# Gathering chosen tokens from a token-major copy: feature order, read stride, and fills on TensorE

## The chip, the cores and the metric

The kernel runs as one program on one core of a Trainium2 chip. The metric is the time of one execution on the device in microseconds. Three runs of the kernel before took 1545.58, 1551.16 and 1552.26 us (median 1551.16). TensorE's clock is granted at one of two levels, 1.2 and 2.4 GHz; a profile shows the second as 1.00 and the first as 0.50.

## The reference

A block of two layers on 256 tokens of 1024 features, all in fp32. The first layer mixes tokens (a gated scan in two directions, a spatial gate, an output projection) and then sends tokens through 16 experts by expert choice:

```python
def moe_expert_choice(h, router_w, w_gate, w_up, w_down):
    B_, T, _ = h.shape
    cap = CAPACITY_FACTOR * T // N_EXPERTS          # 2 * 256 / 16 = 32
    aff = jax.nn.softmax((h @ router_w).astype(jnp.float32), axis=-1)
    gate, idx = lax.top_k(jnp.swapaxes(aff, 1, 2), cap)
    xs = h[bidx, idx]
    hid = jax.nn.silu(jnp.einsum('becd,edf->becf', xs, w_gate)) * jnp.einsum('becd,edf->becf', xs, w_up)
    ye = jnp.einsum('becf,efd->becd', hid, w_down) * gate[..., None].astype(h.dtype)
    return jnp.zeros_like(h).at[bidx, idx].add(ye)
```

`w_gate`, `w_up` and `w_down` are 16 x 1024 x 2048 (or its transpose) each: 8 MB for each expert and matrix, some 403 MB in all. The second layer (a linear-attention branch, a convolution branch, an output projection and a gated extra input) follows.

## The kernel before

Activations are kept by features: feature on the partition, token on the free axis. The projections of both layers are done as three products in a rounded format (weights and activations split into a high and a low part); the experts, the gathers and the scatters are plain fp32, for which the profile has two records a product.

Between the first layer's output projection and the experts lies the choice. `routed(k)` (L1955) computes the logits of the 16 experts and transposes the tokens' features block by block into four PSUM banks, so that a token lies on a partition. ScalarE copies these banks to SBUF, scaled by each token's norm, as `H2k` (L719, four copies of 128x512). VectorE computes the softmax (`affk`, L1260 to L1270), TensorE transposes it (L2057), VectorE takes the 32 largest values of each expert in four rounds and counts them through (L1274 to L1284, event "ranks"), TensorE transposes the ranks back (L2066), and VectorE writes one-hot matrices `Pm` that say which token goes to which of an expert's 32 places (L1291, L1295). In between TensorE has products of its own to do, which belong to the second layer (`pp_products`, L2035): eight records ahead of the transposes of the softmax and 24 behind them. The latter start only when the third copy of `H2k` has emptied its bank, since they write to that bank. Two products without a use, `keep_on(2)` (L2029), stand behind the transposes of the ranks.

The gathers are matrix products: stationary is a 128x128 piece of `H2k` (128 tokens, 128 features), moving is `Pm`. There are eight blocks k of 128 features, and two token halves i:

```python
mm = e.matmul(B[b][:, 0:32], H2k[:, i, 512 * (k // 4) + k % 4:512 * (k // 4) + 512:4], Pm[:, i, 0, :], ...)
```

The slice ends in `:4`: block k takes every fourth feature of a range of 512, because the rows of the expert weights are loaded so that each partition holds four neighbouring rows. The columns of the piece are 16 bytes apart. `gather_first(k)` gathers for expert 0 alone (32 columns), `gather(0, k)` for experts 1 to 7 (224 columns), `gather(1, k)` for experts 8 to 15 (256). ScalarE takes each result to `XS` (L723, L728).

`up(x, m, b)` (L2116) does eight steps k for expert x and matrix m (0 gate, 1 up): four products of 32 stationary columns and 512 moving columns, one for each quarter of 2048 outputs, side by side on the array (eight records). For x = 0, m = 0 each step first issues `gather_first(k + 1)`; for x = 0 and x = 1 with m = 1 each step first issues `gather(x, k)`. The down products (L2165) follow the transposes of `hid`.

The weights come on one queue, issued by SyncE in the order of `LOADS` (L309). The first 20 tiles of 1 MB (24 tiles make an expert: 8 gate, 8 up, 8 down) are loaded ahead of the experts, as far as there is room. Each later load waits until the last tile that lay in its place has been used (`p_exp`, L491): the load of tiles 20 and 21 waits for tile 1, that of 22 and 23 for tile 3, that of 24 and 25 for tile 7, that of 26 and 27 for tile 9, and so on round the ring. Engines have their orders written out by hand, and semaphores join them.

Of the kernel before, what the change touches and what calls it, by code (L numbers as in the profile page):

```python
# [11 lines left out]
ACT = mybir.ActivationFunctionType  # L12
# [52 lines left out]
def program(nc, a, out):  # L65
    ctx = ExitStack()
    with ctx:
        names = []

        def signal(name, step=1):  # L70
            names.append(Signal(ctx.enter_context(nc.semaphore(name)), step))
            return names[-1]
# [7 lines left out]
        def put(name, n, at=None, dtype=F32):  # L80
            o = pos[0] if at is None else at
            if at is None:
                pos[0] = o + (n + 7) // 8 * 8
            assert o + n <= TOT, (name, o, n)
            return nc.alloc_sbuf_tensor_at(name, [128, n], dtype, offset=arena + 4 * o)[:, :]
# [11 lines left out]
        B = [ctx.enter_context(nc.psum_tensor(f"B{i}", [128, 512], F32))[:, :] for i in range(8)]  # L97
# [72 lines left out]
        ffs, ffp, lgb, rsc = put("ffs", 16), put("ffp", 16), put("lgb", 16), put("rsc", 8)  # L170
# [3 lines left out]
        H2k = v2(put("h2k", 2048, page(13)))  # L174
# [3 lines left out]
        Pm = put("pick", 1024).rearrange("p (i e s) -> p i e s", i=2, e=16)  # L178
# [156 lines left out]
        def expert_src(t, n):  # L335
# [49 lines left out]
        a_step, a_hi, a_left, a_sig, a_h, a_lvl, a_norm, a_moe = (signal(n) for n in (  # L385
            "act_step", "act_hi", "act_left_bank", "act_sigmoid", "act_h", "act_level", "act_norm", "act_moe"))
# [126 lines left out]
        def scalar(e):  # L513
# [202 lines left out]
            for c in range(2):  # L716
                for i in range(2):
                    e.wait_ge(*p_misc.at("xt", c))
                    e.activation(H2k[:, i, 512 * c:512 * c + 512], B[2 * c + i], ACT.Copy, scale=rsc[:, i:i + 1]).then_inc(*a_left("h2k", c, i))  # L719

            def gather_first(k):
                e.wait_ge(*p_misc.at("gather first", k))
# [946 lines left out]
        def tensor(e):  # L1669
            left = {}  # L1670

            def bank(b):

                if b in left:
                    e.wait_ge(*left.pop(b))
                return B[b]

            def next_bank(*key):
                b = UNIT_BANK[key]
                return bank(b), b  # L1680
# [24 lines left out]
            def mm3(ps, n, cols, ah, al, kn=8, w_first=True, ready=None):  # L1705

                wh, wl = kn_(hi_(n), n)[:, :, cols], kn_(lo_(n), n)[:, :, cols]
                if n >= SECOND and ready is None:
                    e.wait_ge(*v_lo.at(n))
                    for k in range(kn):  # L1710
                        for j, (w, x) in enumerate(((wh, ah), (wh, al), (wl, ah))):
                            mm = e.matmul(ps, w[:, k, :], x(k), start=k == 0 and j == 0, stop=k == kn - 1 and j == 2)  # L1712
                    return mm
                e.wait_ge(*a_hi.at(n))
                for k in range(kn):
                    if ready is not None:
                        e.wait_ge(*ready(k))
                    for j, x in enumerate((ah, al)):
                        l, r = (wh[:, k, :], x(k)) if w_first else (x(k), wh[:, k, :])
                        e.matmul(ps, l, r, start=k == 0 and j == 0, stop=False)  # L1720
                e.wait_ge(*v_lo.at(n))
                for k in range(kn):
                    l, r = (wl[:, k, :], ah(k)) if w_first else (ah(k), wl[:, k, :])
                    mm = e.matmul(ps, l, r, start=False, stop=k == kn - 1)  # L1724
                return mm

            half = lambda j: slice(128 * j, 128 * j + 128)
# [24 lines left out]
            ps, b = next_bank("q", 0)  # L1752
# [3 lines left out]
            for k in range(8):  # L1756
                e.wait_ge(*v_h.at("lo", 0, k))
                for j in range(2):
                    for i, (w, x) in enumerate(((wh, hx), (wh, hxl), (wl, hx))):
                        mm = e.matmul(ps[:, 256 * j:256 * j + 256], w[:, k, half(j)], x(k), start=k == 0 and j == 0 and i == 0, stop=k == 7 and j == 1 and i == 2)  # L1760
# [13 lines left out]
            for h in range(2):  # L1774
                for k in range(8):
                    mm = e.matmul(two_banks[h], wl[:, k, half(h)], HTh[:, k, :], start=False, stop=k == 7)
# [3 lines left out]
            for d in range(2):  # L1780
                for h in range(4):
# [3 lines left out]
                    ps, b = next_bank("f", d, h)  # L1785
# [106 lines left out]
            for h in range(4):  # L1892
# [10 lines left out]
                mm = e.matmul(po, vx[:, 1, half(h)], PT[:, 1, h, :], start=False, stop=True)  # L1903
# [10 lines left out]
            for g in range(4):  # L1914
# [5 lines left out]
                for i in range(2):  # L1920
                    o0 = 256 * (g % 2) + 128 * i
                    mm = e.matmul(B[4 + g // 2][:, o0:o0 + 128], svt[:, i, half(g)], wst[:, g, :], start=True, stop=True)
# [8 lines left out]
            for b_ in range(4):  # L1931
                for hf in range(4):
                    mm = e.matmul(B[4][32 * hf:32 * hf + 32, 0:16].rearrange("p (m q b) -> p b m q", m=2, b=4)[:, b_], ident[:, b_::4],
                                  ffs.rearrange("p (m q h) -> p h m q", m=2, h=4)[:, hf], start=True, stop=True)
# [5 lines left out]
            for c in range(2):  # L1940
                for name, xh, xl in (("a", oTh, oTl), ("b", uTh, uTl)):
# [3 lines left out]
                    for hf in range(2):  # L1945
                        ps, b = next_bank(name, c, hf)
                        for j in range(2):
                            mm = mm3(ps[:, 256 * j:256 * j + 256], n, half(2 * hf + j), lambda k: xh[:, k, :], lambda k: xl[:, k, :], kn=4)
# [29 lines left out]
            for c in range(4):  # L1978
                n = NO["wo", c]
                if c == 0:  # L1980

                    ps, b = next_bank("wo", 0)
                    e.wait_ge(*v_lo.at(n))
                    wh, wl = kn_(hi_(n), n), kn_(lo_(n), n)
                    for ks in (range(6), (6, 7)):
                        for j in range(2):
                            for k in ks:
# [5 lines left out]
                                mm = e.matmul(pj, wl[:, k, half(j)], mh(k), start=False, stop=k == 7 and j == 1)  # L1993
# [4 lines left out]
                else:  # L1998

                    ps, b = next_bank("wo", 3)  # L2000
# [8 lines left out]
                    for k in range(8):  # L2009
                        mm = e.matmul(ps, wl[:, k, half(1)], mh(k), start=False, stop=k == 7)  # L2010
# [18 lines left out]
            def keep_on(times, b=7):  # L2029

                bank(b)
                for _ in range(times):
                    e.matmul(B[b][:, 0:128], ident, ident, start=True, stop=True)

            def pp_products(c, k):  # L2035
                if k == 0:
                    bank(pp_bank[c])
                for db in (2 * c, 2 * c + 1):
                    pp_product(db, k)

            def pp_product(db, k):
                b = pp_bank[db // 2]
                mm = e.matmul(B[b][:, 256 * (db % 2):256 * (db % 2) + 256], wpp[:, k, half(db)], pT[k], start=k == 0 and db % 2 == 0, stop=k == 1 and db % 2 == 1)
                if k == 0 and db == 7:
                    mm.then_inc(*p_misc("pp", "upper rows"))
                if k == 1 and db % 2:
                    mm.then_inc(*p_misc("pp", db // 2))
                    left[b] = a_left.at("pp", db // 2)
# [2 lines left out]
            e.wait_ge(*l_pT.at(1))  # L2051
            for k in range(2):
                pp_products(0, k)
            bank(5)
            e.wait_ge(*v_moe.at("aff"))
            for i in range(2):
                mm = e.transpose(B[5][0:16, half(i)], affk[:, i, :], ident)  # L2057
            mm.then_inc(*p_misc("aff"))
            left[5] = v_left.at("aff")
            for k in range(2):  # L2060
                for c in range(1, 4):
                    pp_products(c, k)
            e.wait_ge(*v_moe.at("ranks"))
            bank(4)
            for i in range(2):
                mm = e.transpose(B[4][:, 16 * i:16 * i + 16], af[0:16, half(i)], ident[0:16, 0:16])  # L2066
# [4 lines left out]
            def gather_first(k):  # L2071
                b = first_bank(k)
                bank(b)
                if k == 0:
                    e.wait_ge(*v_moe.at("pick first"))
                    e.wait_ge(*a_left.at("h2k", 1, 1))
                for i in range(2):
                    mm = e.matmul(B[b][:, 0:32], H2k[:, i, 512 * (k // 4) + k % 4:512 * (k // 4) + 512:4], Pm[:, i, 0, :], start=i == 0, stop=i == 1)
                mm.then_inc(*p_misc("gather first", k))
                left[b] = a_moe.at("xs first", k)  # L2080

            def gather(hf, k):
                b, c0 = gather_bank(hf, k), 0 if hf else 32
                bank(b)
                if k == 0:
                    e.wait_ge(*v_moe.at("pick", hf, 1))
                for i in range(2):
                    mm = e.matmul(B[b][:, 0:256 - c0], H2k[:, i, 512 * (k // 4) + k % 4:512 * (k // 4) + 512:4], Pm[:, i, 8 * hf + c0 // 32:8 * hf + 8, :], start=i == 0, stop=i == 1)  # L2088
                mm.then_inc(*p_misc("gather", hf, k))
                left[b] = a_moe.at("xs", hf, k)  # L2090

# [43 lines left out]
            for x in range(NE):  # L2135
# [4 lines left out]
                for i in range(2):  # L2140
                    mm = e.transpose(B[7][:, half(i)], PR[:, i, :, :].rearrange("p r s -> p (r s)"), ident)  # L2141
# [6 lines left out]
                for c in range(4):  # L2148
                    mm = e.transpose(B[2][:, half(c)], hid[:, c::4], ident)  # L2149
# [5 lines left out]
                for j in range(4):  # L2155
# [5 lines left out]
                    for i, part in enumerate(parts):  # L2161
                        if t + i == load_of[t][0] or len(parts) == 2:
                            e.wait_ge(*(l_last.at() if i < len(parts) - 1 else landed[tile_page(t)].at("expert", t + i)))
                        for db, c, r in part:
                            mm = e.matmul(B[3 + db][32 * r:32 * r + 32, :], hidT[:, 128 * c + 32 * j:128 * c + 32 * j + 32],  # L2165
                                          v2(tile_at_page(t + c // 2))[:, c % 2, 512 * db:512 * db + 512], start=j == 0, stop=j == 3)
# [201 lines left out]
        for f in (sync, scalar, vector, gpsimd, tensor):  # L2368
            f(Counting())
# [8 lines left out]
        @block.scalar  # L2378
        def _(eng):
            scalar(eng)  # L2380
# [55 lines left out]
```

## Time and profile before

| | |
|---|---|
| Median of three runs | 1551.16 us |
| Profiled execution's own time | 1552.23 us |
| Its span (first to last instruction) | 1550.4 us |
| TensorE matmul busy | 1211.2 us (78%) |
| TensorE weight loads busy | 757.2 us (49%) |
| VectorE, ScalarE, GpSimd busy | 562.5, 423.9, 30.0 us |
| Mean granted clock of TensorE | 0.874 |
| Read from memory | 518.66 MB, 335 GB/s over the span |

Times in the rows below are counted from the span's start. PE is TensorE's matmuls, PEld its weight loads (they run beside matmuls), DVE VectorE, ACT ScalarE, POOL GpSimd, SPq SyncE's queue. L719 is line 719 of the kernel. "B<-pick,h2k" names what an instruction writes and reads. A record of a matmul lasts from its start until its result has drained, so that records overlap; the pace of a row of them is read from the chain of waits or from the starts.

### The profile page before, as it was taken

Reading aid. Unit: us, or ns where it says so; the run is one execution under the profiler, and the core shown is the slowest. Engines: PE = TensorE matmul, PEld = TensorE weight load, DVE = VectorE, ACT = ScalarE, POOL = GpSimd, SP = SyncE. Lnnn points to the kernel's source line nnn. Section 1 sums busy time; section 2 is a strip of 40 time slices with the busy share of each in tenths; the row PEclk is TensorE's granted clock in tenths of the full one; section 3 lists DMA queues with packets and bytes.
Section 4 is the critical chain, followed back from the end, with each engine's and each line's share of the span. In section 5 each row is a group of like instructions: output and inputs, shape, how many; then the busy total and the mean of one; then the engine's idle time right before and its main releaser. Section 6 shows DMA issues by size and latency. Waiting matters only on the chain.

```text
span 1550.4 us, 18533 instructions
## 1 busy us (share of the span) xinstructions
PE 1211.2 (78%) x8124; PEld 757.2 (49%) x8124; DVE 562.5 (36%) x829; ACT 423.9 (27%) x553; POOL 30.0 (2%) x36
## 2 busy tenths in 40 slices
PE   4999999999666756666756656656656899999998
PEld 1878899854212212212211212212212589999997
DVE  4887776511101101101101101101101497777566
ACT  2865656222100000000000000000000454467545
POOL 0012000000000000000000000000000000000000
PEclk7999999979968777867878787878878999999999
DMA  9646868769999999999999999999999855555551
GB/s 364 215 156 224 298 221 332 299 249 424 432 431 431 432 432 431 430 431 431 431 431 430 432 432 432 431 429 430 432 432 427 328 164 163 162 182 184 184 186 55
DMA packets 106479, 520.90 MB, mean 336 GB/s; under 512 B 5904, under 2 KB 83728, under 8 KB 89376
## 3 DMA queue, kind: packets, MB, share of 16 engines
q1 hardware_dynamic: 106256, 519.63, 83.3%
q8 instruction: 64, 1.05, 0.3%
q14 instruction: 15, 0.12, 0.0%
q10 hardware_dynamic: 144, 0.09, 0.0%
HBM read 518.66 MB, written 1.05 MB: 335 GB/s over the span
## 4 chain that ended last, share of the span: by engine, by line
PE 49%; DMA 47%; DVE 1%; ACT 1%; SPq 1%; issue 1%; DVEq 0%
PE B L1712 16%; DMA four<-in_wd 15%; DMA four<-in_wu 15%; DMA four<-in_wg 13%; PE B L2130 8%; PE B L1720 6%; PE B L2165 3%; PE B L1724 3%; PE B L1839 2%; DMA wslot<-in_w_in 2%; PE B L2088 1%; DMA aslot<-in_ada_w 1%; PE B L1690 1%; PE B L1827 1%; PE B L1842 1%; DMA wslot<-in_w_out 1%
## 5 line engine op out<-in xcount | busy, mean ns | idle before, releaser
L2130 PE MATMUL B<-four,xs 128*32 128x512 f32 x1824 | 294.7, 804 | 197.9 <-DMA four<-in_wu 132.5
L2130 PEld LDWEIGHTS B<-four,xs 128*32 128x32 f32 x1824 | 73.4, 141 | 398.4 <-issue 323.5
L2165 PE MATMUL B<-four,hidT 128*32 128x512 f32 x896 | 153.2, 846 | 88.0 <-DMA four<-in_wd 87.4
L1712 PE MATMUL B<-hnh,whj 128*128 128x256 f32 x488 | 138.1, 283 | 0.0
L1712 PE MATMUL B<-hnh,wslot_r 128*128 128x256 f32 x488 | 137.6, 282 | 0.0
L1712 PE MATMUL B<-hn_r,whj 128*128 128x256 f32 x488 | 137.1, 281 | 0.0
L2165 PEld LDWEIGHTS B<-four,hidT 128*32 128x32 f32 x896 | 37.0, 148 | 193.5 <-issue 121.7
L970 DVE TENSOR_TENSOR wslot_r<-wslot,whj 128x2048 fp32r<-128x2048 f32 x52 | 118.8, 2288 | 31.4 <-ACT whj L524 31.3
L524 ACT ACTIVATE whj<-wslot 128x2048 fp32r<-128x2048 f32 x51 | 97.3, 1913 | 87.6 <-PE B L1712 82.0
L1324 DVE TENSOR_TENSOR hid<-sgm,B 128x512 f32<-128x512 f32 x16 | 11.0, 688 | 281.5 <-PE B L2130 281.5
L1304 DVE SCALAR_TENSOR_TENSOR x<-B,mod,x 128x256 f32<-128x256 f32 x128 | 55.9, 479 | 152.6 <-PE B L2106 152.6
L1335 DVE COPY ye<-B 128x512 f32<-128x512 f32 x15 | 10.4, 692 | 262.0 <-PE B L2165 262.0
L1712 PEld LDWEIGHTS B<-hnh,wslot_r 128*128 128x128 f32 x488 | 93.6, 192 | 0.0
L1712 PEld LDWEIGHTS B<-hn_r,whj 128*128 128x128 f32 x488 | 91.8, 188 | 0.1
L1712 PEld LDWEIGHTS B<-hnh,whj 128*128 128x128 f32 x488 | 91.6, 188 | 0.1
L751 ACT ACTIVATE hidT<-B 128x512 f32<-128x512 f32 x16 | 9.6, 597 | 287.5 <-PE B L2149 287.5
L745 ACT ACTIVATE gt<-B 128x256 f32<-128x256 f32 x16 | 6.1, 384 | 259.2 <-PE B L2141 259.2
L760 ACT ACTIVATE ye<-B 128x512 f32<-128x512 f32 x15 | 9.0, 597 | 240.6 <-PE B L2165 240.6
L1720 PE MATMUL B<-hh,whi 128*128 128x256 f32 (+1 forms) x256 | 71.0, 308 | 0.0
L970 DVE TENSOR_TENSOR wslot_r<-wslot,whi 128x2048 fp32r<-128x2048 f32 x29 | 66.3, 2285 | 12.8 <-ACT whi L524 10.5
L1720 PE MATMUL B<-h_r,whi 128*128 128x256 f32 (+1 forms) x256 | 69.6, 303 | 0.0
L2106 PE MATMUL B<-gt,ye 128*128 128x256 f32 x256 | 63.5, 391 | 1.6
(509 smaller groups left out, 1970.0 us busy)
## 6 DMA issues: line engine op xcount, KB each, us to landing
four<-in_wu SPq DMA_DIRECT2D x29, 4096.0 KB, 33.5
four<-in_wd SPq DMA_DIRECT2D x28, 4096.0 KB, 34.0
four<-in_wg SPq DMA_DIRECT2D x28, 4096.0 KB, 32.7
wslot<-in_w_in SPq DMA_DIRECT2D x58, 1024.0 KB, 5.2
aslot<-in_ada_w SPq DMA_DIRECT2D x20, 1024.0 KB, 7.4
pair<-in_wg SPq DMA_DIRECT2D x8, 2048.0 KB, 9.3
pair<-in_wu SPq DMA_DIRECT2D x6, 2048.0 KB, 11.9
pair<-in_wd SPq DMA_DIRECT2D x6, 2048.0 KB, 14.4
```

What stands on the lines that cost most here:

```text
L524: e.activation(hi_(n), raw(n), ACT.Copy).then_inc(*a_hi(n))
L970: e.tensor_tensor(lo_(n), raw(n), hi_(n).bitcast(F32), ALU.subtract).then_inc(*v_lo(n))
L1304: e.scalar_tensor_tensor(XX[:, db, :], B[scat_bank(x, db // 2)][:, 256 * (db % 2):256 * (db % 2) + 256], mod[:, 40 + db, 0:1], XX[:, db, : ...
L1690: mm = e.matmul(B[0][32 * j:32 * j + 32, :], csil[:, k, :], slots[s][:, 512 * j:512 * j + 512], start=k == 0, stop=k == 7)
L1712: mm = e.matmul(ps, w[:, k, :], x(k), start=k == 0 and j == 0, stop=k == kn - 1 and j == 2)
L1720: e.matmul(ps, l, r, start=k == 0 and j == 0, stop=False)
L1724: mm = e.matmul(ps, l, r, start=False, stop=k == kn - 1)
L1827: mm = e.matmul(B[4 + j][:, half(h)], K0[:, h, half(j)], Q0[:, h, half(i)], start=True, stop=True)
L1839: e.matmul(ps, x[:, 4 * half_k + k, tk], wh[:, k, :], start=half_k == 0 and k == 0 and x is ah, stop=False)
L2106: mm = e.matmul(B[b][:, 256 * j:256 * j + 256], YE[:, half(db)], Gt, start=True, stop=True)
L2130: mm = e.matmul(B[b][32 * j:32 * j + 32, :], XS[x // 8][:, k, 32 * (x % 8):32 * (x % 8) + 32], columns(t, j), start=k == 0, stop=k == 7)
L2165: mm = e.matmul(B[3 + db][32 * r:32 * r + 32, :], hidT[:, 128 * c + 32 * j:128 * c + 32 * j + 32], v2(tile_at_page(t + c // 2))[:, c % 2, ...
```

## The change

Three edits.

The copy of `H2k` reads its bank in another order: from each range of 512 features it reads every fourth feature and writes these side by side, so block k of the gathers is 128 neighbouring columns. The gathers then read that block with no step. And two products without a use are issued twice more: ahead of the transposes of the softmax, and behind them, ahead of the 24 records of `pp_products`.

```diff
@@ scalar
             for c in range(2):
                 for i in range(2):
                     e.wait_ge(*p_misc.at("xt", c))
-                    e.activation(H2k[:, i, 512 * c:512 * c + 512], B[2 * c + i], ACT.Copy, scale=rsc[:, i:i + 1]).then_inc(*a_left("h2k", c, i))
+                    e.activation(H2k[:, i, 512 * c:512 * c + 512].rearrange("p (k q) -> p k q", k=4), B[2 * c + i].rearrange("p (q k) -> p k q", k=4),
+                                 ACT.Copy, scale=rsc[:, i:i + 1]).then_inc(*a_left("h2k", c, i))
@@ tensor
             for k in range(2):
                 pp_products(0, k)
+            keep_on(2)
             bank(5)
             e.wait_ge(*v_moe.at("aff"))
             for i in range(2):
                 mm = e.transpose(B[5][0:16, half(i)], affk[:, i, :], ident)
             mm.then_inc(*p_misc("aff"))
             left[5] = v_left.at("aff")
+            keep_on(2)
             for k in range(2):
                 for c in range(1, 4):
                     pp_products(c, k)
@@ gather_first
-                    mm = e.matmul(B[b][:, 0:32], H2k[:, i, 512 * (k // 4) + k % 4:512 * (k // 4) + 512:4], Pm[:, i, 0, :], start=i == 0, stop=i == 1)
+                    mm = e.matmul(B[b][:, 0:32], H2k[:, i, half(k)], Pm[:, i, 0, :], start=i == 0, stop=i == 1)
@@ gather
-                    mm = e.matmul(B[b][:, 0:256 - c0], H2k[:, i, 512 * (k // 4) + k % 4:512 * (k // 4) + 512:4], Pm[:, i, 8 * hf + c0 // 32:8 * hf + 8, :], start=i == 0, stop=i == 1)
+                    mm = e.matmul(B[b][:, 0:256 - c0], H2k[:, i, half(k)], Pm[:, i, 8 * hf + c0 // 32:8 * hf + 8, :], start=i == 0, stop=i == 1)
```

`half(k)` is the slice from 128 k to 128 k + 128.

## Rows read from the trace of the kernel before

**Rows 1.** Page, the span in 40 slices: granted clock, and GB/s moved.
```profile
PEclk7999999979968777867878787878878999999999
GB/s 364 215 156 224 298 221 332 299 249 424 432 431 431 432 432 431 430 431 431 431 431 430 432 432 432 431 429 430 432 432 427 328 164 163 162 182 184 184 186 55
```
**Rows 2.** Page, chain that ended last: shares of the span by engine.
```profile
PE 49%; DMA 47%; DVE 1%; ACT 1%; SPq 1%; issue 1%; DVEq 0%
```
**Rows 3.** Busy time by stretch (x: instructions), granted clock, DMA share, GB/s.
```profile
core 0: us, PE busy (x) PEld busy (x) DVE busy (x) ACT busy (x) POOL busy (x), PEclk, DMA share, GB/s
313.90:317.70 3.80, 3.80 (x22) 2.89 (x20) 1.26 (x4) 0.76 (x2) 0.61 (x1) 1.00 0.00 0
317.70:320.00 2.30, 2.30 (x11) 0.57 (x10) 0.00 (x0) 0.38 (x1) 0.00 (x0) 0.51 0.00 0
320.00:321.70 1.70, 1.70 (x8) 1.06 (x12) 0.00 (x0) 0.38 (x1) 0.00 (x0) 0.50 0.83 154
321.70:336.30 14.60, 14.60 (x65) 5.28 (x57) 0.00 (x0) 3.57 (x8) 0.00 (x0) 0.50 0.68 270
336.30:338.20 1.90, 1.90 (x10) 1.48 (x6) 0.69 (x1) 1.18 (x3) 0.62 (x1) 0.50 0.58 138
338.20:354.90 16.70, 16.65 (x93) 8.33 (x92) 0.69 (x1) 5.27 (x10) 0.00 (x0) 1.00 0.98 392
354.90:400.00 45.10, 41.17 (x282) 18.30 (x282) 7.00 (x14) 8.56 (x15) 0.62 (x1) 1.00 1.01 429
400.00:1190.00 790.00, 498.95 (x2896) 155.36 (x2896) 86.65 (x167) 49.21 (x83) 7.99 (x13) 0.79 1.00 431
```
**Rows 4.** Chain of waits in order of time, 303 to 355 us: start, us, what.
```profile
303.88 0.36 PE B L1975 x4
...
305.94 1.74 ACT h2k L719 x3
...
313.39 0.64 PE B L2033 x4
314.04 1.95 PE B L2078 x8
...
316.98 1.07 PE B L2078 x4
318.06 1.87 PE B L2130 x8
...
332.76 3.57 PE B L2130 x16
...
340.62 1.00 PE B L2130 x8
341.61 1.21 PE B L2088 x4
```
**Rows 5.** Loads issued by SyncE, in order of time: start, us, what.
```profile
319.98 6.21 SPq L445 DMA_DIRECT2D pair<-in_wd  x2
336.39 14.44 SPq L445 DMA_DIRECT2D pair<-in_wg  x4
```
**Rows 6.** Groups, shapes apart, 296 to 345 us: busy us, mean ns.
```profile
L2078 PEld LDWEIGHTS B<-pick,h2k 128*128 128x128 f32 x32 | 8.0, 325 | 9.2 <-issue 8.3 <-ACT xs L723 0.8
L719 ACT ACTIVATE h2k<-B,rsc 128x512 f32<-128x512 f32 x4 | 2.4, 683 | 0.0
L1964 PEld LDWEIGHTS B<-wrs,x 128*128 128x128 f32 x16 | 2.1, 191 | 0.3 <-DVE x L1243 0.3
```
**Rows 7.** The same, 12 to 42 us, where the clock was low.
```profile
L1750 PE MATMUL B<-ident 128*128 128x128 f32 x16 | 3.6, 417 | 0.0
```
**Rows 8.** TensorE's matmuls in order of time: start, us, what, idle before it.
```profile
306.73 0.38 PE L2057 MATMUL B<-ident,affk 128*16 128x128 f32 x2 [0.67 <-DVE affk L1270]
307.72 5.45 PE L2043 MATMUL B<-pT,wpp 128*128 128x256 f32 x24 [0.61 <-ACT h2k L719]
...
410.32 5.11 PE L2130 MATMUL B<-four,xs 128*32 128x512 f32 x32 [6.16 <-DMA four<-in_wg]
```

## The prediction

> **What bounds the kernel now.** I read the slices of the page first. From about 349 to 1190 us the queue moves 424 to 432 GB/s in nearly every slice, flat [rows 1]; over 400 to 1190 us the DMA engines are busy all the time at 431 GB/s while TensorE works 499 of 790 us [rows 3]. There nothing but bytes counts. Ahead of it and behind it the chain runs through TensorE, which is why the whole chain is split 49% PE and 47% DMA [rows 2]. The place to look at is the seam: the slice 310 to 349 us has 249 GB/s [rows 1]. The table of stretches opens it up: 0 GB/s from 313.9 to 320.0, 154, then 270 until 336.3, 138, then 392 until 354.9, and 429 from there on [rows 3]. The queue isn't slow there, it has no place to write to: it issues two loads at and behind 319.98, and the next only at 336.39 [rows 5]. Those are the moments at which tiles 1 and 7 had been used. So in this seam TensorE's speed through expert 0's gate products sets when the DMA stream starts, and the stream then carries each microsecond won or lost to 1190 us.
>
> What does TensorE do there? The chain of waits shows it alternating: four records of the gather 1.07 us, eight of the gate products 1.87 us, in all 2.94 us a step, from 316.98 on [rows 4]. Two things are odd. The gate products take 1.87 us here and 1.00 us at 340.62 [rows 4]: the granted clock is 1.00 up to 317.7, 0.50 from there to 338.2 and 1.00 again behind it, that is 1.2 and not 2.4 GHz [rows 3]. And the clock fell while TensorE was "busy" all of 313.9 to 317.7 [rows 3]. What it did in that stretch was mostly gathers: twelve records with 32 moving columns each, and one set of gate products. Secondly the gathers themselves: eight take 1.95 us at the full clock, 0.24 us each, and four take 1.07 us at the half [rows 4], the same pace at both clocks. They are held by their weight loads, which last 325 ns for 128 columns that lie 16 bytes apart, against 191 ns for 128 columns side by side (L1964) [rows 6].
>
> **The change part by part.** The sum is made against the profiled execution, 1552.23 us; it lies 1.1 us over the median of the runs shown, so the forecast needs no correction for a lucky profile.
>
> *Gathers with neighbouring columns.* Four records with neighbouring stationary columns and few moving ones (L1975, one column) take 0.36 us at the full clock; four with 128 moving columns (L2033) 0.64 us, of which a part is the change of kind [rows 4]. 32 moving columns lie nearer to the first; I take 0.37 us for a step's four records in place of 1.07.
>
> *The clock.* Now each step at full clock is 0.37 us of gather and 1.00 us of gate products. Gate products are 73% of the time, where at the fall they were about a quarter. The stretch 338.2 to 354.9 us has 1.00 us of them in each 2.21 us, the rest gathers with 224 columns, and it held the full clock throughout [rows 3, 4]. So I expect that the full clock is kept through the seam; this is the likeliest case and half of the gain.
>
> *The sum at TensorE.* Gather 0 starts at 314.04. The gate products of step 0 need ScalarE's copy of gather 0 (0.38 us), which could start about 0.4 us after the gather's start and not, as before, about 1.05: they start at some 314.95 and not 315.99. Then eight steps of 1.00 and six gathers of 0.37: 314.95 + 8.0 + 2.2 = 325.15 for the end of tile 7, where before it was 332.76 + 3.57 = 336.33 [rows 4]: 11.2 us earlier. Tile 1 is done at 314.95 + 1.00 + 0.37 + 1.00 = 317.3 and not 319.9: 2.6 us earlier.
>
> *What this does to the stream.* From 313.9 to 354.9 us the queue moved 154 x 1.7 + 270 x 14.6 + 138 x 1.9 + 392 x 16.7 = 11.0 MB [rows 3]. At the 431 GB/s of later that is 25.6 us out of 41.0: 15.4 us were lost. After the change the load for tiles 20 and 21 is issued at 317.3; before, issued at 319.98, it had moved only 0.26 MB by 321.7, so I count 1.1 us from issue to full flow. The stream then starts at 318.4, with 4.5 us lost. The next loads come at tile 3 (about 320.1) and tile 7 (325.2), each while the one before it, 2 MB or some 4.9 us, still runs (318.4 to 328.2 for two), and tile 9, 11 and so on follow at 0.37 to 0.9 us of gather and 1.0 of products a tile, under 4 us for two, faster than the queue moves them. So it should not break off again. Gain: 15.4 - 4.5 = 10.9 us. The row of 392 GB/s shows that pairs may run below 431: if all eight pairs (16.8 MB) moved at 392, they would be through at 318.4 + 42.8 = 361.2, where before they are at 354.9 + 5.8 MB / 429 = 368.4, a gain of 7.2. I take 10.5, near the upper end, since two loads will be outstanding where in that row there was mostly one.
>
> *The later gathers.* 16 steps take 1.21 us of gather (L2088) [rows 4]; with the pace of L2043, whose 24 records with 256 columns take 5.45 us, four take 0.91 [rows 8], so 0.3 us each, 4.8 in all. They lie under a saturated stream in the forecast and are counted at nothing. If the stream had holes there, as before at 392 GB/s, up to half (the eight of expert 0, 2.4 us) would count.
>
> *The copies of H2k.* Four copies at 683 ns [rows 6]; the third ends at 307.68 and lets go the 24 records [rows 4, 8], which end at 313.2, later than the ranks of VectorE. So a slower copy is on the path three times over. No copy with a step of 16 bytes in PSUM stands in the trace. From below: nothing (a reason for a gain isn't to be seen, the same 512 elements a partition). From above, by the nearest row, the weight loads with that very step at 325 against 191 ns, a factor 1.7 [rows 6]: 0.48 us more a copy, 1.4 us in all. I take 0.1 us a copy, 0.3 us in all, because ScalarE takes one element at a time in any case.
>
> Here the Trainium skill speaks against the change. Its page "SBUF — State Buffer", section "Door 1: The DMA port swizzle", says that PSUM is organised in lines of 8 bytes and that "any non-contiguous PSUM access pattern significantly slows down matmuls"; the edit moves the step of 16 bytes from SBUF into PSUM. By the same passage a step of 16 bytes in SBUF also gets one fp32 a line, which agrees with 325 against 191 ns [rows 6]. No row shows the PSUM side.
>
> *The two fills.* Two products of L2033 are 0.64 us [rows 4]. The first stands in the 0.67 us in which TensorE waited for the softmax, the second in the 0.61 us in which it waited for the third copy [rows 8]. Cover is complete, up to 0.1 us; if it were gone they would cost 1.3 us. Bank 7, to which they write, was last read long before. Their worth here is nil, since the clock was held over 306 to 314 us in this execution; they would matter where it is not.
>
> Sum: 1552.2 - 10.5 + 0.3 + 0.1 = 1542.1. Nothing is moved past another queue: no load, wait or instruction of SyncE, GpSimd or VectorE changes its place. What is late next is the stream itself.
>
> **The rivals.**
>
> *B, the clock falls all the same.* TensorE called busy on weight loads did not hold it once. For: the ranks' transposes, the start and the short wait for ScalarE still thin out 313 to 316 us. Against: the share worked out above. Price: step 0 at full clock, then seven sets of 1.87 us and six gathers. Neighbouring columns at 1.2 GHz: 16 records took 3.6 us (L1750), four 0.9 [rows 7]; from below twice 0.36 less the change of kind, 0.6. Tile 7 ends at 314.95 + 1.0 + 13.1 + 3.6 to 5.4 = 332.6 to 334.5, 2 to 4 us early. The stream breaks off as before until then, so this is the gain: 1552.2 + 0.4 - 3.0 = 1549.6.
>
> *C, the step costs nothing in itself.* The 325 ns would then be something else about L2078, such as its 32 moving columns. Against: L1964, with 16, has 191. Price: no change at the gathers, the clock falls as before, 1552.5. The Trainium skill's page "TensorE: Matmul & The Clock Gate", section "LDWEIGHTS (loading the stationary operand)", gives a weight load's time by its number of columns alone; by that rule this is what would happen. The trace disagrees, 325 against 191 ns for the same 128 columns.
>
> *D, slower: ScalarE's copy becomes what everything waits for, and takes the clock with it.* If a copy takes 1.1 us more, the 24 records start 3.3 us later, with TensorE idle but for a fill. After an idle time of 6.16 us in the expert stage the clock was low: 32 records took 5.11 us [rows 8], between the 4.0 of the full clock and the 7.1 of the low one (four times 1.00, twice 3.57) [rows 4]. Then the 24 records take up to 5.2 us more, and the seam goes as in B: 1549.6 + 3.3 + 5.2 = 1558.1. Without the fall the dear copy leaves 1542.1 + 3.0 = 1545.1. So it decides from a copy about 1 us dearer on; the row that I have bounds it at 0.5.
>
> **How the numbers follow.** Forecast (full clock kept) 0.74, B 0.15, C 0.03, D 0.05 (a dear copy with the fall), 0.03 for the rest. In the forecast's case the stream's two bounds give 1541.7 to 1545.4, the copies up to 1.4 more; a load that flows at once and later gathers that count take it down to 1539. Range 1539 to 1549, which leaves out D, C and half of B. What a measurement of this kernel can tell from no change is 0.5%, 7.8 us: under 1543.4 is faster. Of the forecast's 0.74 four fifths lie there, and a little of the rest: faster 0.60. B, C and the upper part of the forecast: same 0.33. D and half of the rest: slower 0.07.
>
> **What would show it.** Weight loads of L2078 near 191 ns. A granted clock of 1.00 over 314 to 338 us. Tile 7 done at 325 and the third issue of SyncE there. The queue at 0 GB/s for some 5 us and then over 420. The 24 records starting at 307.7 to 308.1 (copies at 0.68 to 0.8 us). From 400 us on all should be the same pattern, 10 us early. I am wrong if the clock falls in the seam, if a copy takes over 1.1 us, or if the stream, started earlier, breaks off or runs near 392 GB/s.

## The result and the profile after

| | runs | median | lowest to highest |
|---|---|---|---|
| before, beside the change | 8 | 1545.53 us | 1545.21 to 1552.28 |
| after | 8 | 1542.63 us | 1541.26 to 1543.28 |

The ratio of after to before is on record as 0.995 (95% interval 0.9933 to 0.9967); the two medians of this table alone give 0.998. The forecast, 1542.1 us, hit the time of the kernel after to 0.5 us. It missed the gain: against the median of 1551.16 us that was known it said 9.1 us, and beside the change the kernel before took 1545.53, so the measured gain was 2.9 us. That is under the 0.5% (7.8 us) that the prediction took as the least that can be told from no change. The cause lies with the kernel before: its times fall into two groups. Of the three times that I knew, two belong to the upper group, and so does the profiled execution; four of the five new ones belong to the lower.

The profiled execution after took 1543.28 us (span 1541.5). Its stretches, with the same bounds as [rows 3] (columns: TensorE's matmuls, its weight loads, VectorE, ScalarE, GpSimd, granted clock, DMA share, GB/s):
```profile
core 0: us, PE busy (x) PEld busy (x) DVE busy (x) ACT busy (x) POOL busy (x), PEclk, DMA share, GB/s
313.90:317.70 3.80, 3.69 (x31) 2.47 (x34) 1.69 (x6) 0.76 (x2) 0.62 (x1) 1.00 0.02 6
317.70:320.00 2.30, 2.30 (x20) 0.75 (x20) 0.00 (x0) 0.76 (x2) 0.00 (x0) 1.00 0.47 93
320.00:321.70 1.70, 1.70 (x16) 0.68 (x12) 0.00 (x0) 0.38 (x1) 0.00 (x0) 1.00 0.56 193
321.70:336.30 14.60, 14.60 (x106) 6.59 (x106) 1.38 (x2) 7.42 (x16) 0.61 (x1) 1.00 1.00 426
...
338.20:354.90 16.70, 15.13 (x128) 5.22 (x131) 1.38 (x2) 2.81 (x5) 0.00 (x0) 1.00 1.00 427
...
400.00:1190.00 790.00, 493.96 (x2896) 155.21 (x2896) 85.95 (x166) 48.60 (x82) 7.99 (x13) 0.79 1.00 431
```
The clock is 1.00 all through the seam, and the stream, once it runs, runs at 426 and 427 GB/s where it had 270 and 392. Summed over 313.9 to 354.9 us with the row left out (457 GB/s for 1.9 us) it moved 14.8 MB and not 11.0. At 431 GB/s that is 6.7 us lost and not 15.4: 8.7 us won, and the two profiled executions differ by 8.95 us.

The chain of waits through the seam, start and us, beside [rows 4]:
```profile
306.87 1.74 ACT h2k L719 x3
...
308.66 5.45 PE B L2044 x24
314.10 0.22 PE B L2069 x2
314.32 0.64 PE B L2034 x4
314.97 0.98 PE B L2081 x8
315.95 0.12 issue
316.06 1.06 PE B L2133 x8
317.13 0.56 PE B L2081 x4
317.69 0.99 PE B L2133 x8
...
325.48 1.85 PE B L2133 x16
327.33 0.37 PE B L2144 x2
327.70 0.76 PE B L2091 x4
...
329.45 0.95 PE B L2091 x4
```
A step is 0.56 + 0.99 us, where it was 1.07 + 1.87. The seam begins 0.93 us later (314.97 against 314.04), as do the copies of H2k (306.87 against 305.94): that was lost ahead of the change's place. In the execution after again the seam begins at 313.52, so this is the spread of single executions. The end of tile 7 is 327.33 against 336.33. Counted from its own start the seam lasts 12.36 us to the end of tile 7, where it lasted 22.29.

The loads that SyncE issues, beside [rows 5]: the first waits for tile 1, and comes at 318.75 where it came at 319.98; the next line begins at the end of tile 7, at 327.39 where it was 336.39.
```profile
318.75 3.44 SPq L445 DMA_DIRECT2D pair<-in_wd  x2
327.39 12.20 SPq L445 DMA_DIRECT2D pair<-in_wg  x4
```
The moments ahead of the seam, beside [rows 8]: TensorE's idle times of 0.67 and 0.61 us are down to 0.22 and 0.17 behind the two added fills (L2034).
```profile
307.66 0.38 PE L2059 MATMUL B<-ident,affk 128*16 128x128 f32 x2 [0.22 <-DVE affk L1271]
307.88 0.61 PE L2034 MATMUL B<-ident 128*128 128x128 f32 x4
308.66 1.13 PE L2044 MATMUL B<-pT,wpp 128*128 128x256 f32 x4 [0.17 <-ACT h2k L719]
```
And the groups, shapes apart, beside [rows 6]: the weight load of a gather lasts 190 ns (325 before), that of L1965 191 ns as before, and the copy, which now reads every fourth element of its PSUM bank, 683 ns as before.
```profile
L2081 PEld LDWEIGHTS B<-pick,h2k 128*128 128x128 f32 x32 | 4.1, 190 | 5.1 <-ACT xs L724 5.0
L719 ACT ACTIVATE h2k<-B,rsc 128x512 f32<-128x512 f32 x4 | 2.4, 683 | 0.0
L1965 PEld LDWEIGHTS B<-wrs,x 128*128 128x128 f32 x16 | 2.1, 191 | 0.3 <-DVE x L1244 0.3
```

### The profile page after: what moved, and what is told of

It reads as the page before. It is cut to its first block, busy times and chain, and to the rows that moved or that the text cites. A ratio compares the mean times of both kernels' runs of the same rounds, so it can differ in the third digit from the quotient of the medians.

```text
span 1541.5 us, 18549 instructions
## 1 busy us (share of the span) xinstructions
PE 1194.6 (77%) x8132; PEld 748.5 (49%) x8132; DVE 562.5 (36%) x829; ACT 423.8 (27%) x553; POOL 30.0 (2%) x36
## 3 DMA queue, kind: packets, MB, share of 16 engines
q8 instruction: 64, 1.05, 0.3%
HBM read 518.66 MB, written 1.05 MB: 337 GB/s over the span
## 4 chain that ended last, share of the span: by engine, by line
PE 49%; DMA 47%; DVE 2%; ACT 1%; SPq 1%; issue 1%; DVEq 0%
PE B L1713 16%; DMA four<-in_wd 16%; DMA four<-in_wu 15%; DMA four<-in_wg 13%; PE B L2133 7%; PE B L1721 6%; PE B L2168 3%; PE B L1725 3%; PE B L1840 2%; DMA wslot<-in_w_in 2%; PE B L1691 1%; PE B L1828 1%; PE B L2091 1%; PE B L1843 1%; DMA wslot<-in_w_out 1%; DMA wslot<-in_ada_w 1%
```

## The experiments

Three sets of four kernels, each set on one chip beside the kernel before. "Lower" counts runs of the lower group, "upper" those of the upper one; the bounds of the groups are given with each.

| run | its median | runs, lower / upper | before beside it |
|---|---|---|---|
| before again | 1549.41 | 6 / 6 | 1551.72 (23 runs) |
| stride only | 1541.83 | 6 / 0 | 1551.72 |
| fills only | 1551.91 | 1 / 11 | 1551.72 |
| later gathers strided | 1541.61 | 6 / 0 | 1551.72 |
| strided, held | 1548.00 | 11 / 1 | 1551.80 (29 runs) |
| thin ahead | 1551.41 | 0 / 12 | 1551.80 |
| no fills | 1542.50 | 9 / 3 | 1551.80 |
| loads split | 1541.48 | 6 / 0 | 1551.80 |
| after again | 1541.70 | 9 / 0 | 1551.28 (21 runs) |
| stride only again | 1542.03 | 9 / 0 | 1551.28 |
| without the old fill | 1541.63 | 8 / 0 | 1551.28 |
| loads split again | 1541.24 | 7 / 0 | 1551.28 |

**The kernel before, once more.** No edit.

> The kernel before, once more, for its own spread: earlier runs lie at 1545.2 to 1545.6 and at 1551.2 to 1552.3, with nothing between. Theory (clock): the two groups are executions whose clock stays at 2.4 GHz for most of the seam (gathers and gate products of expert 0) and executions in which it falls there. Then a run at 1545.4 has a mean granted clock about 0.006 higher than one at 1552, and a profile of it shows gate products at 1.00 us a step and not 1.87, with gathers still at 1.07. Rival (stream): the groups come from the DMA side; then the mean clock of the runs doesn't separate them, and a 1545 profile has the same 1.87 us steps.

Six runs lay at 1545.2 to 1547.4 and six at 1551.5 to 1552.8. Their mean clocks are 0.882 to 0.890 and 0.874 to 0.882: all six lower runs lie above five of the six upper ones, so here the clock separates the groups nearly. Over the 85 executions of this kernel in the three sets the mean is 0.888 in the lower group and 0.880 in the upper one, but the two ranges overlap (0.882 to 0.891 and 0.872 to 0.887). The profile caught a run of 1545.24 us, and its chain settles what differs:
```profile
313.41 1.95 PE B L2078 x8
315.36 1.00 PE B L2130 x8
316.36 1.05 PE B L2078 x4
317.41 0.99 PE B L2130 x8
...
327.64 1.85 PE B L2130 x16
329.50 0.37 PE B L2141 x2
```
```profile
321.70:336.30 14.60, 14.60 (x91) 7.52 (x83) 1.38 (x2) 7.29 (x15) 0.61 (x1) 1.00 0.99 389
```
It is the same program, with gathers as slow as ever (1.05 us) and gate products at the full clock. Tile 7 is done at 329.50, 6.8 us before [rows 4]'s 336.33, and the run is 7.0 us shorter. Of the 6.8 us, 0.6 are an earlier start of the seam (313.41 against 314.04); the rest, 6.2, is the clock: seven sets of gate products at 0.99 us in place of 1.87. The stream ran at 389 GB/s over 321.7 to 336.3 in place of 270. So one and the same kernel has executions whose clock holds and executions whose clock falls, and their times are those of the two groups (one profile of each). Over all 93 executions of this kernel, beside the change and in the three sets, 29 lay at 1544.3 to 1547.6 (median 1545.58) and 64 at 1550.2 to 1554.8 (median 1551.90).

**Only the copy and the gathers**, both added fills out.
```diff
                 pp_products(0, k)
-            keep_on(2)
...
             left[5] = v_left.at("aff")
-            keep_on(2)
```

> Copy and gathers changed, both added fills left out. Theory: the fills lie in idle time of a stretch whose clock was held anyway, so 1541.3 to 1543.3 as with the whole change, gathers at 0.56 us a step, clock 1.00 in the seam. Rival: the fills are what keeps the clock up; then some runs lie 4 to 7 us higher.

1541.26 to 1543.15, ratio to before 0.9939 (0.9926 to 0.9952). The read step alone brings what the whole change brings. Repeated in the third set:

> Copy and gathers changed, the two added fills left out, again, for the share of runs in which the clock falls. Without any fill 3 of 12 runs lay at 1549. Theory: the fill behind the ranks' transposes holds the clock, the added two don't matter: all at 1541.2 to 1543.4. Rival: the added two matter in some executions; then one to three of twelve at 1548 to 1550.

Nine runs at 1541.33 to 1542.86, none higher: 15 of 15 with the step removed and the added fills absent.

**Only the fills**, gathers strided.
```diff
                 pp_products(0, k)
+            keep_on(2)
...
             left[5] = v_left.at("aff")
+            keep_on(2)
```

> Both fills added, gathers still read every fourth column. Theory: nothing is gained; 1545.3 in most runs and about 1552 in others, gathers at 1.07 us a step. Rival: the fills remove the upper group; then all runs at 1545.4 and none at 1552, so that part of the change's worth is the fills'.

One run at 1545.41, eleven at 1550.7 to 1552.8; ratio 1.0001 (0.9989 to 1.0013). Nothing is gained. I had expected 1545.3 in most runs; eleven of twelve were in the upper group. In the profiled one (1551.61 us) the clock fell in the seam and the steps are 1.07 + 1.86 us.

**Later gathers strided.** As after, but the 16 later gathers take every fourth column of the new copy and so gather other features.
```diff
-                    mm = e.matmul(B[b][:, 0:256 - c0], H2k[:, i, half(k)], ...
+                    mm = e.matmul(B[b][:, 0:256 - c0], H2k[:, i, 512 * (k // 4) + k % 4:512 * (k // 4) + 512:4], ...
```

> As the whole change, but the 16 later gathers (experts 1 to 15) read every fourth column of the new copy, and so take other features than the reference wants; only their time is meant. Theory: they lie under the saturated stream and cost nothing, 1541.3 to 1543.3 as with the whole change, though TensorE is some 5 us later at the end of them. Rival: the stream is held up by them; then 1544 to 1547.

1541.43 to 1543.01. Their gathers take the old time:
```profile
327.36 1.00 PE B L2133 x8
328.35 1.21 PE B L2091 x4
```
with the stream at 428 GB/s over 336.3 to 354.9 us all the same. The later gathers are worth nothing here, as counted; only expert 0's eight matter.

**Strided, held.** The kernel before, with one fill product behind each of seven gathers of expert 0.
```diff
                             gather_first(k + 1)
+                            keep_on(1, 4)
```

> The kernel before (gathers read every fourth column), with one fill product (0.22 us) behind each of seven of expert 0's gathers, to hold the clock. Theory (the two groups of the kernel before are one kernel with and without the clock's fall in the seam, worth 6 to 7 us): all runs in one group, 1545.4 plus up to 1.6 us for the fills, so 1545.5 to 1547.2, none at 1551 or above, and the seam's steps at full clock. What is left to the whole change, 4 to 5 us, is then the read step alone. Rival: the groups have another cause, and there are still runs at 1551 and above.

Eleven runs at 1546.5 to 1549.2, one at 1555.88; beside it the kernel before had 6 of 29 runs in its lower group. So with fills in the seam the clock may have fallen in one run of twelve, where 23 of the 29 beside it lay in the upper group. The fills cost more than I expected, 0.30 us each and not 0.22, 2.1 in all, and the median of 1548.0 is 2.4 above the lower group's. One chain line of the profile shows such a fill, and its neighbours the full clock:
```profile
318.11 0.30 PE B L2033 x2
318.41 0.99 PE B L2131 x8
319.41 1.05 PE B L2078 x4
```

**Thin ahead.** As after, with the 24 records ahead of the ranks moving 8 columns and not 256 (most of that product is left out).
```diff
-                mm = e.matmul(B[b][:, 256 * (db % 2):256 * (db % 2) + 256], wpp[:, k, half(db)], pT[k], ...
+                n_ = 256 if db < 2 else 8
+                mm = e.matmul(B[b][:, 256 * (db % 2):256 * (db % 2) + n_], wpp[:, k, half(db)], pT[k][:, 0:n_], ...
```

> The whole change, but the 24 records ahead of the ranks move 8 columns and not 256, so most of the second layer's small product is left out: TensorE does much less just ahead of the seam. Theory: the clock then falls before or in the seam, and gathers with neighbouring columns don't save it; gate products at 1.87 us a step, gathers at 0.7 to 0.9, tile 7 done 6 to 8 us later than in the whole change: 1547 to 1550 in most runs. Rival (it was the read step alone that cost, the clock costs little in the seam): 1541 to 1543, or up to 0.7 us less, since the gathers start sooner.

All twelve runs at 1548.3 to 1552.3. TensorE had less to do ahead of the seam. The clock fell at some 311 us, where the shortened records end, and TensorE then stood idle for 1.78 us until the transposes of the ranks. The change was worth nearly nothing:
```profile
310.00:313.90 3.90, 2.12 (x16) 1.99 (x16) 3.21 (x11) 0.00 (x0) 0.00 (x0) 0.65 0.68 286
313.90:317.70 3.80, 3.80 (x19) 2.21 (x18) 1.21 (x4) 0.76 (x2) 0.62 (x1) 0.50 0.01 4
```
```profile
317.91 0.99 PE B L2082 x4
318.90 1.87 PE B L2134 x8
```
At 1.2 GHz four records of a gather with neighbouring columns take 0.99 us, at most 0.08 less than the strided ones. The weight loads last 333 ns there (288 to 338), with neighbouring columns, as the strided ones of before do. So nearly all of the step's worth is at the full clock. This is rival B's low clock made to happen, with the fall some 3 us ahead of the seam and an idle time between them; rival B had it fall in the seam, with TensorE busy. The price of a gather is above the one I gave it.

**No fills.** As after, with both added fills out and the old one behind the ranks' transposes out as well.
```diff
             left[4] = v_left.at("ranks")
-            keep_on(2)
```

> The whole change without any fill, the one behind the ranks' transposes left out too. Theory: that fill lies beside VectorE's 0.6 us for the first one-hot matrix, and the clock holds by the gate products; 1541.2 to 1543.2 as with the change. Rival: the fills hold the clock; then a group of runs at 1546 or above.

Nine runs at 1541.2 to 1543.5, three at 1548.9 to 1549.4. My theory fell in part: without any fill the upper group is back in a quarter of the runs. The price, 7 us, is near that of a fallen clock, but the profile caught a lower run, and the mean clocks of the three (0.880 to 0.887) don't stand out from the others' (0.881 to 0.888), so the fall itself isn't shown for them. Which fill it is, the next one asks: the two added fills kept, the old one out.

> The whole change with its two added fills, but without the old fill behind the ranks' transposes. Theory: it is this old fill, just ahead of the gathers, that holds the clock; then 2 to 4 of 12 runs lie at 1548 to 1550, as without any fill, the rest at 1541.2 to 1543.4. Rival (any of the fills does it): all at 1541.2 to 1543.4.

Eight runs at 1540.7 to 1541.9 (a ninth execution, of 3716 us, was disturbed and is left out). So neither fill alone is needed: the old one alone gave 15 of 15, the added two alone 8 of 8, none 9 of 12. With counts this small, three in twelve against none in fifteen is a hint and not more. Taken together the kernels with neighbouring gathers and at least one of the fills have 59 runs (8 + 9 of the whole change, 15, 8, 6 with strided later gathers, 13 with loads split), and none lies above 1543.5; that makes three in twelve without any more than a hint, though only six of the 59 ran on its chip.

**Loads split.** As after; the loads of tiles 20 to 25 wait and go tile by tile.
```diff
+                elif t in (20, 22, 24):
+                    n, r = load[1:]
+                    for j in range(2):
+                        e.wait_ge(*p_exp.at("tile", before(load) - 1 + j))
+                        e.dma_start(homes[n, r][:, j * SLOT:(j + 1) * SLOT], expert_src(t, 2)[:, j * SLOT:(j + 1) * SLOT]).then_inc(...)
+                    continue
```

> The whole change, and the loads of tiles 20 to 25 issued a tile at a time, each as soon as the one tile under it has been used, not in pairs. Theory (the end is set by when the stream starts again): the first megabyte can start when tile 0 is done, 1.6 us earlier, and the end comes 1.6 us earlier: 1539.7 to 1541.5. Rival (the stream's own speed, or TensorE behind it, sets the end): no gain, or a loss by smaller transfers, 1541.3 to 1544.

> Loads of tiles 20 to 25 issued a tile at a time, again, now on one chip with the whole change. From the first look, where its median was 1541.5: 0.5 to 1.5 us less than the whole change beside it. Rival (nothing gained): within 0.3 us of it.

1541.48, then 1541.24 us beside 1541.70 for the whole change on the same chip. The stream does start earlier, as over 317.7 to 321.7 us in the last set (291 and 354 GB/s), after again first, then loads split again:
```profile
317.70:321.70 4.00, 4.00 (x33) 1.51 (x32) 0.00 (x0) 1.14 (x3) 0.00 (x0) 1.00 0.88 291
```
```profile
317.70:321.70 4.00, 4.00 (x33) 1.49 (x32) 0.00 (x0) 1.14 (x3) 0.00 (x0) 1.00 0.90 354
```
Only 0.5 us of the expected 1.6 comes out at the end, within the spread of single runs, so this isn't shown to be faster. The two profiles say where the rest is given back. The chain's last load of `w_up` lands at 1179.63 in loads split again and at 1181.16 in after again, still 1.5 us early. Then it waits for the second layer's first weights (`in_w_in`), 26.55 us and not 25.38, which are there at 1213.02 and 1213.37 us, only 0.35 us early, about the difference of the two runs' times. Why that load takes longer stays open. 1541.24 is the lowest median of all kernels tried.

**The whole change again.**

> The whole change again, beside more executions of the kernel before. Theory (two groups before, one after): all runs at 1541.2 to 1543.4; the kernel before again has about a third of its runs at 1544 to 1548 and the rest at 1550 to 1554, so its median lies near 1551.7 and the ratio at 0.994. Rival (the change has a second group too, not met in eight runs): some runs at 1548 or above.

Nine runs at 1540.9 to 1543.4; with the first eight, 17 of 17 in one group, median 1541.74. The kernel before had 7 of 21 in its lower group. The ratio was 0.9954 (0.9937 to 0.9971); in the set of the stride alone it was 0.9939.

## Why the prediction was right and wrong

**What bounds the kernel: right.** The seam's speed sets when the stream starts, and what is won there is kept to the end. Before again won 6.8 us at tile 7 and 7.0 at the end; after against before won 9.0 at tile 7 and 8.95 at the end. Loads split, where 1.1 us of the 1.5 was lost behind the experts, shows that this isn't so for every microsecond.

**The failed step: "it lies 1.1 us over the median of the runs shown, so the forecast needs no correction for a lucky profile".** It treated 1545.58, 1551.16 and 1552.26 as one spread. They are two groups 6.3 us apart, and the profile lay in the upper one. The forecast's sum starts from 1552.2 and counts "the clock" as half of its gain; that half exists only against an execution whose clock falls. Against the upper group (1551.90) the change is worth 10.2 us, against the lower one (1545.58) 3.8. A median of eight runs with five in the lower group is 1545.53; this makes 5.6 of the 6.2 us between 9.1 and 2.9, and 0.5 is the time of after. Which group such a median falls into is luck: with 23, 29 and 21 executions of before the medians were 1551.72, 1551.80 and 1551.28. The lowest of the three times that I was shown, 1545.58, was the sign. A strided seam at the full clock would have accounted for it: from 315.99 us on, eight sets of gate products of 1.00 us and six gathers of 1.07 end at 330.4 in place of 336.33, 5.9 us early.

**Gathers: the right mechanism, a term mis-sized.** "I take 0.37 us for a step's four records": measured 0.56. I went by L1975, with one moving column. A step's four records take 0.14 us each, which is nearer to the 0.16 of L2033. Six steps of 0.19 more are 1.1 us of the sum at TensorE: the seam took 12.36 us and not 11.1. The weight load did go from 325 to 190 ns, so rival C is out, and with it, for fp32 at the full clock, the rule that the number of columns alone counts. That 1542.1 lies so near to the 1542.63 measured, and to 1541.74 over all 17 runs, is in part luck: the 1.1 us were covered by the 0.4 us set aside for copies and fills, which cost nothing, and by taking 10.5 us of the 11.2 at TensorE.

**Clock kept: right for the kernel after.** Both of its profiles show it, and all 17 runs lie in one group. That the clock falls with strided gathers is shown only as something that may go either way (before against before again); which executions fall wasn't controlled. Strided, held has 11 of 12 runs below 1549.2, so products put between such gathers help. Why neighbouring columns keep the clock, the larger share of gate products or something else, isn't shown.

**Copies: right, and the bound too wide.** 683 ns before and after. The warning of the Trainium skill's page "SBUF — State Buffer", section "Door 1: The DMA port swizzle", speaks of matmuls; it doesn't reach ScalarE here, whose read of PSUM with a step of 16 bytes cost nothing.

**Fills: half right.** In this change they bring nothing that shows (stride only is as fast). "Cover is complete" holds: behind the fills TensorE still waits 0.22 and 0.17 us. The prediction called their worth nil with the clock held and added that "they would matter where it is not"; the second half deserved more weight: no fills had three upper runs of twelve, the kernels with any of the fills none of 59.

**Later gathers at nothing: right** (later strided). **Stream near 431 and not 392 GB/s: right,** 426 and 427. That the 392 of before came from single loads with nothing queued behind fits this but wasn't tested by itself (before again, with gathers as slow but the clock kept, has 422 GB/s over 338.2 to 354.9 us).

**Rival B** was priced at 0.6 to 0.9 us a gather at the low clock; thin ahead shows 0.99. With that, tile 7 would end at 314.95 + 1.0 + 13.1 + 5.9 = 335.0, some 1.4 us early and not 2 to 4 (an estimate). None of the 17 runs of after shows it. The three upper runs of no fills, 1548.9 to 1549.4, lie where rival B was put (1549.6), but none of them was profiled.

## What to carry to other kernels

Before a profile is used as a baseline, put its time beside all run times and ask whether they form one group. If they don't, work out the change against each group, since a change that removes a chance of a low clock is worth a different amount against each group, and the median of a few runs is a matter of the draw. In this kernel the clock was lost in a stretch with 12 gather records of few moving columns, with TensorE busy 3.80 of 3.80 us, so a busy engine is no proof that the clock will hold. In such a stretch the order in which the stationary operand is stored is cheap to change if the engine that copies it can reorder for nothing.

## What the runs showed of the hardware

- Reading 512 fp32 of a PSUM bank with a step of four elements cost ScalarE the same 683 ns as reading them in order.
- A weight load of 128 fp32 columns 16 bytes apart lasts 325 ns at either clock, and four records of a gather take 1.05 us at 2.4 GHz and 1.07 at 1.2. With neighbouring columns the load lasts 190 ns and the four take 0.56 us at 2.4 GHz, but 333 ns and 0.99 us at 1.2 GHz. So at the low clock the step costs at most 0.08 us of four records, and at the full clock it takes the gather back to the low clock's pace.
- One program has two groups of times, 6.3 us apart, by one fall of the clock in a stretch of some 20 us ahead of a saturated stream: 1.87 for 0.99 us a set of gate products, seven times.
